# Squares of each MLP's first up unit on ScalarE, and a later start of the four raw weight buffers

## What is computed

```python
mod = (jax.nn.silu(c) @ ada_w[i] + ada_b[i]).reshape(c.shape[0], N_MOD, D_MODEL)
...
hn = modulate(x, norm_g[i, 1], mod[:, 3], mod[:, 4])
f = jnp.square(jax.nn.relu(hn @ mlp_w_up[i])) @ mlp_w_down[i]
x = x + mod[:, 5][:, None, :] * f
```

## Time and profile before

| | |
|---|---|
| median of three runs | 1337.34 us (1335.83 to 1338.08) |
| the profiled execution | 1337.55 us, span 1335.8 us, mean granted clock 0.991 |
| busy: PE, DVE, ACT, POOL | 96%, 61%, 36%, 31% |
| HBM read and written | 160.70 MB and 6.94 MB, 125 GB/s over the span |
| chain that ended last | PE 79%, DVE 12%, issue 4%, ACT 3% |

### The profile page before, as it was taken

One profiled execution on the slowest core, in us unless ns is written; L12 is line 12 of the kernel. 1 busy time (PEld: TensorE's weight loads), 2 busy tenths in 40 slices (PEclk: granted clock), 3 DMA queues, 4 the chain that ended last, 5 costly groups with the idle time before them and its releaser, 6 DMA issues.

```text
span 1335.8 us, 26336 instructions
## 1 busy us (share of the span) xinstructions
PE 1288.0 (96%) x11305; PEld 1254.0 (94%) x11305; DVE 811.4 (61%) x1312; ACT 485.5 (36%) x760; POOL 412.3 (31%) x200
## 2 busy tenths in 40 slices
PE   5899999999999999999999999999999999999996
PEld 4799999999989999999999999999999999999996
DVE  2623435667978642742649809859898643734764
ACT  3532442222422451451463322223322461642721
POOL 2434434443342032032035344435243032050050
PEclk9899999999999999999999999999999999999998
DMA  9666214754464465465463232323232242342321
GB/s 333 198 195 161 78 54 119 225 164 123 147 197 148 147 200 158 136 213 158 127 192 95 59 100 82 93 82 95 64 96 64 64 127 64 96 127 58 101 64 67
DMA packets 239806, 169.34 MB, mean 127 GB/s; under 512 B 5691, under 2 KB 211775, under 8 KB 239562
## 3 DMA queue, kind: packets, MB, share of 16 engines
q1 hardware_dynamic: 215946, 121.33, 31.6%
q10 hardware_dynamic: 23584, 46.27, 10.5%
q0 software_dynamic: 160, 0.07, 0.0%
HBM read 160.70 MB, written 6.94 MB: 125 GB/s over the span
## 4 chain that ended last, share of the span: by engine, by line
PE 79%; DVE 12%; issue 4%; ACT 3%; DMA 1%; POOL 0%; SPq 0%; ACTq 0%; POOLq 0%; DVEq 0%
PE G L1851 39%; PE G L1971 16%; PE G L1877 9%; PE G L2001 5%; PE B L2023 4%; DVE hb L1332 1%; DVE acc L1209 1%; PE B L1837 1%; DVE small_s L1778 1%; DVE yc L1777 1%; DVE Hh L1170 1%; DMA xin<-in_x_sample 1%; DVE Xl L1346 1%; PE B L2190 1%; DMA batch<-in_ada_w 1%
## 5 line engine op out<-in xcount | busy, mean ns | idle before, releaser
L1030 POOL TENSOR_TENSOR wl<-raw,wh 128x1024 fp32r<-128x1024 f32 x144 | 371.7, 2589 | 764.8 <-ACT wh L553 761.8
L553 ACT ACTIVATE wh<-raw 128x1024 fp32r<-128x1024 f32 x144 | 152.1, 1056 | 275.5 <-PE G L1851 137.0
L1851 PE MATMUL G<-Hh,wh 128*128 128x272 f32 x864 | 180.6, 290 | 3.5 <-DVE xT L1193 3.5
L1851 PE MATMUL G<-Hh,wl 128*128 128x272 f32 x864 | 179.0, 289 | 0.0
L1851 PE MATMUL G<-Hl,wh 128*128 128x272 f32 x864 | 178.7, 288 | 0.0
L1851 PE MATMUL G<-Xh,wh 128*128 128x272 f32 x672 | 145.1, 297 | 1.2 <-POOL wl L1030 1.2
L1851 PEld LDWEIGHTS G<-Hh,wh 128*128 128x128 f32 x864 | 136.2, 189 | 5.7 <-issue 5.7
L1851 PE MATMUL G<-Xl,wh 128*128 128x272 f32 x672 | 139.3, 289 | 0.0
L1851 PE MATMUL G<-Xh,wl 128*128 128x272 f32 x672 | 138.6, 288 | 0.0
L1851 PEld LDWEIGHTS G<-Hl,wh 128*128 128x128 f32 x864 | 136.5, 189 | 0.0
L1851 PEld LDWEIGHTS G<-Hh,wl 128*128 128x128 f32 x864 | 135.5, 189 | 0.0
(11 more groups left out here) (377 smaller groups left out, 2756.0 us busy)
## 6 DMA issues: line engine op xcount, KB each, us to landing
aring<-in_ada_w ACTq DMA_DIRECT2D x70, 512.0 KB, 5.2
raw<-in_mlp_w_up SPq DMA_DIRECT2D x64, 512.0 KB, 4.4
raw<-in_mlp_w_down SPq DMA_DIRECT2D x64, 512.0 KB, 4.4
raw<-in_mlstm_w_in SPq DMA_DIRECT2D x24, 512.0 KB, 4.2
raw<-in_conv_w_in SPq DMA_DIRECT2D x24, 512.0 KB, 3.8
early<-in_ada_w SPq DMA_DIRECT2D x16, 512.0 KB, 12.4
raw<-in_mlstm_w_out SPq DMA_DIRECT2D x8, 512.0 KB, 5.2
batch<-in_ada_w ACTq DMA_DIRECT2D x8, 512.0 KB, 6.3
```

The lines of the kernel that those rows point to most:

```text
L553: nc.scalar.activation(wh[:, t % SLOTS], raw_of(t), ACT.Copy).then_inc(s_hi, 1)
L1030: nc.gpsimd.tensor_tensor(wl[:, t % SLOTS], raw_of(t), wh[:, t % SLOTS].bitcast(F32), ALU.subtract).then_inc(s_lo, 1)
L1851: last = mm(G[:, 2 * (g % 2) + hf, 0:HALF], w[:, s, k, :], x[:, k, hf * HALF:(hf + 1) * HALF], start=st, stop=en)
```

## The change

It does two things. First, in the first up unit of both MLPs, ScalarE makes both squares: one rounded into `Hh` and one in place in the buffer that holds the ReLU's result, the second only after the first is done. VectorE keeps one subtraction for each tile. The squares stand ahead of the evictions of tiles 35 to 39 (131 to 135), as `SQUARE_AT` has them, and the last behind. The wait for the state stores and the normalisers moves to ScalarE's first square, since `Hh` lies where the state was. Second, `T_RAW4` becomes 48, so that tiles 40 to 47 go through the two buffers.

```diff
-T_RAW4 = T_MLP0 + 8
+T_RAW4 = T_MLP0L
+SQUARE_AT = {3: (0,), 4: (1, 2), 5: (3,), 6: (4,), 7: (5, 6)}
...
                 for m in range(FIRST, KT):
                     hi(t0 + m + LEAD)
+                    if squares is not None:
+                        for i in SQUARE_AT[m]:
+                            first_square(squares, g0, i)
                     evac(t0 + m, g0 + m, None, 0, 0)
                     if ada is not None and m < KT - 1:
                         batch_next(ada, m - FIRST)
+                if squares is not None:
+                    first_square(squares, g0, KT - 1)
+
+            def first_square(v, g0, m):
+
+                act.wait_ge(s_ev, done(g0 + m + 1))
+                if m == 0 and v == 0:
+                    act.wait_ge(s_out, 16 * STORES_STATE)
+                    act.wait_ge(s_nfin, 1)
+                s = scaled_in(m, g0 + m)
+                chain.link(nc.scalar.activation(Hh[:, m, :], s, ACT.Square))
+                nc.scalar.activation(s, s, ACT.Square).then_inc(s_usq, 1)
...
-            first_unit(1, T_MLP0, G_MLP0, 0, 1, first_relu, to_own(ACT.Relu), ada=5)
+            first_unit(1, T_MLP0, G_MLP0, 0, 1, first_relu, to_own(ACT.Relu), ada=5, squares=0)
...
-                    first_unit(3, T_MLP1, G_MLP1, 1, 1, first_relu, to_own(ACT.Relu))
+                    first_unit(3, T_MLP1, G_MLP1, 1, 1, first_relu, to_own(ACT.Relu), squares=1)
...
+            def first_low(v, g0):
+
+                for m in range(KT):
+                    dve.wait_ge(s_usq, KT * v + m + 1)
+                    dve.wait_ge(s_dr, done(g0 + m))
+                    src = OWN.get(m, stage[(g0 + m) % 2])
+                    V.tensor_tensor(Hl[:, m, :], src[:, :], Hh[:, m, :].bitcast(F32), ALU.subtract).then_inc(s_dr, 1)
...
-            unit(G_MLP0, drain_square(Hh, Hl, None, True))
+            first_low(0, G_MLP0)
...
-                    unit(G_MLP1, drain_square(Hh, Hl, None, True))
+                    first_low(1, G_MLP1)
```

More of the change, by code:

```diff
@@ L372, in build_program @@
         s_tf, s_thi, s_tlo = sem("x_sums"), sem("x_sums_hi"), sem("x_sums_lo")
+        s_usq = sem("first_squared")
         s_gn, s_xph, s_xp, s_xps, s_sc = sem("gain_ready"), sem("raw_x_high"), sem("raw_x"), sem("raw_x_samples"), sem("first_tiles_scaled")
@@ L708, in raw_hi, with first_unit @@
                     .then_inc(s_xph, 1)
-            def first_unit(n, t0, g0, layer, which, finish, evac, after={}, ada=None):
+            def first_unit(n, t0, g0, layer, which, finish, evac, after={}, ada=None, squares=None):
                 raw_hi(n, KT - 1)
@@ L1158, in mid, with drain_square @@
                 dve.wait_ge(s_mid, mids["n"])
-            def drain_square(hi_out, lo_out, other, scaled=False):
-                def drain(m, g, j, per):
[L1163 to L1168, removed]
+            def first_low(v, g0):
[4 more added lines that the diff above has]
+                    V.tensor_tensor(Hl[:, m, :], src[:, :], Hh[:, m, :].bitcast(F32), ALU.subtract).then_inc(s_dr, 1)
+            def drain_square(hi_out, lo_out, other):
+                def drain(m, g, j, per):
+                    dve.wait_ge(s_used, at(g + 1, j, per))
+                    ps, o = slot(g), halves(other[:, m, :])
                     dve.wait_ge(s_dr, at(g, j, per))
                     V.tensor_tensor(halves(hi_out[:, m, :]), ps, o, ALU.mult)
[L1171 to L1176, removed]
+                    V.tensor_tensor(halves(sqb[:, :]), ps, o, ALU.mult).then_inc(s_ev, 1)
+                    dve.wait_ge(s_ev, at(g + 1, j, per))
                     V.tensor_tensor(lo_out[:, m, :], sqb[:, :], hi_out[:, m, :].bitcast(F32), ALU.subtract)\
```

## The result

| | before | after |
|---|---|---|
| median | 1337.71 us (1335.83 to 1338.37) | 1330.29 us (1328.74 to 1331.52) |
| profiled execution, span, clock | 1337.55, 1335.8 us, 0.991 | 1330.44, 1328.7 us, 0.994 |
| ACT busy | 485.5 us, 36% | 504.2 us, 38% |
| DVE busy | 811.4 us, 61% | 780.0 us, 59% |

The ratio is 0.9946, with a 95% interval from 0.9929 to 0.9963: faster by 7.4 us. The forecast was 1331.6 in a range from 1328.9 to 1335.6.

What follows compares the result with a forecast made beforehand. TensorE, 96 per cent busy, was taken to bound the kernel, so only its waits and their clock cost could be gained: 2.8 + 1.0 + 1.9 = 5.7 us off the median 1337.34 gives 1331.6 us, range 1328.9 to 1335.6.

Steps and rivals of the forecast that it cites:

- Both waits that it named: TensorE's waits of 3.2 us for the last `ada_w` batch (first MLP) and 2.4 us for ScalarE's eviction (second MLP).
- the two that it let stand: TensorE's two waits for VectorE's residual after the changed stages, 3.5 us together, counted as bringing no gain.
- The squares' price: On ScalarE, 32 added squares of 128x544 at 0.65 us each, 1.4 us a tile with the wait between the two.
- The first pair's cover: First MLP, square pair ahead of tile 35's eviction: costs TensorE nothing at tile 37, with 0.9 us of cover.
- The eviction in the second MLP: Last up tile's eviction follows TensorE directly, no longer late VectorE: wait falls from 2.4 to 0.5 us, gain 1.9.
- The batch: First MLP: fewer raw tiles in the way of the last `ada_w` pieces, TensorE waits 0.4 us, gain 2.8.
- the last pair can't: First MLP: the last batch pair can't go out sooner, since it follows tile 38's eviction; issue stays near 370.3.
- The clock at the batch: First MLP: with the shorter wait the clock stays at 1.00 in the 128 batch matmuls, 4.3 us; gain 1.0.
- The rule on the queues: Packet-by-packet turns give raw tiles an estimated fifth: at most 1.6 us given back, wait left 1.6, sum smaller by 1.2.
- Two buffers: From tile 42 on, two raw buffers cost nothing: 12.1 us for two tiles against 12.2 of TensorE and 1.1 of `ada_w`.
- The second fall of the clock: Rival: after the second MLP's residual wait the clock stays up, 1.8 us more gained, 1329.8 us; chance 0.17.
- the sum of 5.7: Total gain forecast: 2.8 batch wait, 1.0 clock at the batch matmuls, 1.9 eviction wait in the second MLP.

Runs made afterwards that it cites:

- the squares alone: Squares on ScalarE in both MLPs as in the changed kernel, four raw buffers from tile 40 as before: 1336.25 us beside 1337.85, ratio 0.9985.
- the buffers alone: The kernel before with only the two raw buffers up to tile 47, squares still on VectorE: 1334.32 us, ratio 0.9969.

## Why the prediction was right, and where it was not

**What bounds the kernel.** Right. Both waits that it named shrank, the two that it let stand stood, and in the first pair of profiles TensorE's row accounts for the difference to 0.3 us.

**The squares' price.** Right: taken 0.65 and 1.4 us a tile, measured 0.64 and 0.66, a pair 1.3. ScalarE's busy time rose by some 19 us (21 expected). VectorE's fell by 31; 23 was the lower bound, since some of its products ran beside GpSimd, as the one of 2.90 us in the earlier trace rows. The first pair's cover held: the eviction of tile 35 follows the squares, and no wait of TensorE stands at tile 37.

**The eviction in the second MLP.** Right in place and cause, too small in size: 2.38 gained, not 1.9. I left 0.5 for the eviction itself by a border elsewhere; here TensorE has the pair's first step to run meanwhile, and nothing is left.

**The batch.** The size, 2.8, was right in the first profile (2.72) and lucky in that: the waits of 1.67 and 2.12 in the other two leave a gain of 1.5 and 1.1 against the one profile before. The road to it was wrong in part. I had raw tile 40 land sooner through the raw buffers, so that the third pair goes out near 365. It did go out at 365.63, but with the squares alone it did so too (365.58): the squares hold the second pair back to 360.62, 2.3 us behind the issue of raw tile 40 (358.28), where it was 0.4 behind it before (358.12 and 357.68), and raw tile 40 comes sooner. The gain doesn't hang on it: with the buffers alone the third pair stays at 367.76 and the gain is all there. The step that holds is the next one, how many bytes stand beside the last four pieces. Also wrong was "the last pair can't" move. It went out 1.6 us later than before, half of it because tile 38 itself ended later and half behind the high part of tile 41, which I hadn't placed in ScalarE's order. What that costs is not shown: the wait was 0.49 and 2.12 us in the executions with it, and 1.67 in the one without.

**The clock at the batch.** Mis-sized: 1.57 for the 1.0 that I took. Four groups of 1.08 overstate the row at the full clock: 128 in a row take 3.70. And the gain isn't there each time: behind the stop of 2.12 us the matmuls took 5.37.

**The rule on the queues.** By the Trainium skill ("DMA: Bandwidth & Descriptors", "Queues, rings and completion order") each engine takes turns between queues packet by packet. My estimate from it, that raw tiles could give back 1.6 us at most, came out too low: taking 1.26 MB of them out gave back 2.6 us. It took for granted that both queues have packets in line on every engine all the time. In 12.2 us of full engines 3886 raw packets passed beside 1088 of the batch, 48 per cent of the bytes, but not in a steady ratio: 658 beside 999 in 370 to 376.2, 3228 beside 89 in the rest. So the trace shows that the estimate fails; whether the turns themselves do is not shown.

**Two buffers.** Right that they cost TensorE nothing: no wait for a low part. Not foreseen was SP's queue: the two stores of the normalisers that stand behind its raw loads go out at 399.65 in place of 385.14. Nobody waits for them there.

**The second fall of the clock.** I gave it 0.17 as a case of its own, on the premise that one wait less decides. It differs from execution to execution: gone in two of three profiles of the changed kernel. The measured 1330.29 lies between the forecast (1331.6) and that rival (1329.8), as such a mixture would. By the first profile the sum of 5.7 was short by 0.6 for the batch's clock and 0.5 for the eviction, which gives 1330.5. By the mean of the three profiles against the one before it is 1.8 for the batch's wait, 1.0 for its clock, 2.4 for the eviction and 1.1 for the second fall, 6.3 in all; what is missing to the 7.4 between the medians is less than the spread of the runs, and no cause for it is shown. That the forecast came so near is in part luck: the batch counted for more than in two of three profiles, the second fall for nothing.

## What to carry to other kernels

When a DMA is late on full engines, count the bytes that are in line beside it before you look at when it was issued: here holding back two prefetches took 2.6 us off the wait, and issuing a pair 1.6 us earlier nothing. After an edit to the order, read every queue once more, since the last issue may now stand behind something new. A short stop of TensorE has a price beyond its length that comes in some executions and not in others, so don't read a clock gain off a single profile.

## What was not expected of the hardware

The same stop of 2.4 us in the same program costs 1.4 to 1.5 us of clock or nothing. Over the timed executions the clock goes with the time: the ten of the kernel with the squares alone reach from 1332.30 us at a mean clock of 0.995 to 1338.36 at 0.988. One such fall is a quarter of those 6 us; where the rest arises is not shown. And a raw tile's landing, 4.3 us at best, took up to 13.6 us with the squares alone. The wait of the changed kernel for its batch was 0.5, 1.7 and 2.1 us in three executions; the order in which raw tiles and batch pass differs among them, but which difference makes the wait stays open.
